# Values' products between the halves of the keys in two decode turns; first norm's sums ahead of the parameters; first values behind gate tiles

## What is computed

```python
h = rmsnorm(x, norm_mix)
proj = h @ w_in        # q, k, v, z, xbc, dt, glu, and 3 x 1024 gate columns
...                    # sample: keys and values of 1024 past positions from pages of 128
z = jnp.einsum('bqhd,bkhd->bhqk', qblk, k) * scale + bias
log_1mb = jnp.where(mask, jax.nn.log_sigmoid(-z), 0.0)
after = lax.cumsum(log_1mb, axis=3, reverse=True) - log_1mb
w = jnp.where(mask, jnp.exp(jax.nn.log_sigmoid(z) + after), 0.0)
out = jnp.einsum('bhqk,bkhd->bqhd', w, v)
...
gates = jax.nn.sigmoid(proj[..., OFF_GATE:].reshape(b, L, N_BRANCH, D_MODEL))
merged = jnp.einsum('blnd,nbld->bld', gates, u)
```

## Time and profile before

| | |
|---|---|
| time of three runs | 910.25, 917.35, 919.32 us (median 917.35) |
| the profiled execution | 910.75 us, of which 909.0 us from first to last instruction |
| PE / weight loads on PE / DVE / ACT / POOL busy | 834.7 / 507.6 / 406.0 / 224.2 / 132.2 us |
| DMA | 190.37 MB, mean 209 GB/s |
| chain of work that ended last | PE 60%, POOL 11%, SP's queue 9%, DVE 7%, issue 4%, DMA 3% |

### The profile page before, as it was taken

One profiled execution on the slowest core, in us unless ns is written; L12 is line 12 of the kernel. 1 busy time (PEld: TensorE's weight loads), 2 busy tenths in 40 slices (PEclk: granted clock), 3 DMA queues, 4 the chain that ended last, 5 costly groups with the idle time before them and its releaser, 6 DMA issues.

```text
span 909.0 us, 12228 instructions
## 1 busy us (share of the span) xinstructions
PE 834.7 (92%) x4488; PEld 507.6 (56%) x4488; DVE 406.0 (45%) x974; ACT 224.2 (25%) x448; POOL 132.2 (15%) x253
## 2 busy tenths in 40 slices
PE   4899999999778989999789999799999999999895
PEld 2577666766556655756347767563444444433474
DVE  2307664467376464342213411713455354454553
ACT  2211534323332243333032012420111111100233
POOL 4002069999200000000000020000000000000000
PEclk9999999999989999999799999989999999999998
DMA  9423312323872445888575100098998998999701
GB/s 266 105 93 133 134 42 92 116 94 94 264 223 68 133 146 194 268 265 268 157 287 198 46 1 1 1 409 351 397 422 334 421 421 362 421 370 424 295 0 61
DMA packets 80047, 190.37 MB, mean 209 GB/s; under 512 B 9033, under 2 KB 33929, under 8 KB 67687
## 3 DMA queue, kind: packets, MB, share of 16 engines
q1 hardware_dynamic: 78034, 184.50, 55.0%
q0 software_dynamic: 1600, 4.34, 1.7%
q10 hardware_dynamic: 349, 0.70, 0.3%
HBM read 184.23 MB, written 5.64 MB: 209 GB/s over the span
## 4 chain that ended last, share of the span: by engine, by line
PE 60%; POOL 11%; SPq 9%; DVE 7%; issue 4%; DMA 3%; ACT 3%; ACTq 0%; DVEq 0%; POOLq 0%
PE bank L2283 13%; POOL ring L646 8%; PE bank L1731 7%; PE bank L2303 7%; PE bank L2080 6%; PE bank L1904 5%; SPq L413 4%; SPq L410 4%; PE bank L2120 4%; PE bank L2194 4%; PE bank L2247 3%; POOL proj L649 2%; DMA ring<-in_state_cf_conv 2%; DMA gate_w<-in_w_in 1%; PE bank L2224 1%
## 5 line engine op out<-in xcount | busy, mean ns | idle before, releaser
L1731 PE MATMUL bank<-scratch,ring 128*128 128x320 f32 x512 | 144.3, 439 | 0.0
L1904 PE MATMUL bank<-scratch,gate_w 128*128 128x320 f32 x384 | 116.4, 460 | 16.0 <-DMA gate_w<-in_w_in 14.7
L2283 PE MATMUL bank<-weights,h_exp 128*64 128x512 f32 (+1 forms) x864 | 126.8, 492 | 1.2 <-DVE rows L1593 1.2
L1731 PEld LDWEIGHTS bank<-scratch,ring 128*128 128x128 f32 x512 | 96.5, 192 | 43.1 <-issue 5.5
L1904 PEld LDWEIGHTS bank<-scratch,gate_w 128*128 128x128 f32 x384 | 76.1, 203 | 50.6 <-DMA gate_w<-in_w_in 16.1
L1600 DVE TENSOR_TENSOR x<-x,bank 128x320 f32<-128x320 f32 x160 | 67.1, 481 | 52.2 <-PE bank L2247 52.2
L2283 PEld LDWEIGHTS bank<-weights,h_exp 128*64 128x64 f32 (+1 forms) x864 | 39.3, 122 | 65.5 <-issue 57.1
L646 POOL TENSOR_SCALAR ring<-scratch,par_w 128x64 f32<-128x64 f32 x120 | 73.1, 637 | 3.0
L2303 PE MATMUL bank<-weights,act_ft 128*64 128x512 f32 (+1 forms) x432 | 61.0, 486 | 0.4 <-DVE act_ft L1617 0.4
L1184 DVE SCALAR_TENSOR_TENSOR proj<-scratch,par_w,proj 128x256 f32<-128x256 f32 x120 | 53.9, 513 | 0.2
L672 POOL MEMSET scratch<- 16x2048 f32 x1 | 1.8, 1794 | 288.8 <-DVE proj L1455 288.8
(11 more groups left out here) (369 smaller groups left out, 1085.9 us busy)
## 6 DMA issues: line engine op xcount, KB each, us to landing
weights<-in_w_expert_gate SPq DMA_DIRECT2D x32, 1024.0 KB, 10.2
weights<-in_w_expert_up SPq DMA_DIRECT2D x32, 1024.0 KB, 12.2
weights<-in_w_expert_down SPq DMA_DIRECT2D x16, 2048.0 KB, 15.3
ring<-in_w_in SPq DMA_DIRECT2D x8, 2048.0 KB, 7.7
ring<-in_cache_k SPq DMA_DIRECT2D x64, 256.0 KB, 3.9
ring<-in_cache_v SPq DMA_DIRECT2D x64, 256.0 KB, 4.1
gate_w<-in_w_in SPq DMA_DIRECT2D x24, 512.0 KB, 6.3
ring<-in_w_branch SPq DMA_DIRECT2D x3, 2048.0 KB, 8.6
```

Source lines behind the costliest of these rows:

```text
L1731: m = MM(bank[b_][:, 0:T], slot(j, DC, GROUP)[:, k, (n % 4) * P:(n % 4 + 1) * P], h[:, k, :], start=k == 0, stop=k == DC - 1)
L1904: m = MM(bank[b_][:, c0:c0 + T], g_w[GW_AT[g]][:, k, :], h[:, k, :], start=k == 0, stop=k == DC - 1)
L2283: m = MM(bank[0][per * p:per * (p + 1), 0:2 * DE // g], h_exp[i % 2][:, k, first_place(n):first_place(n) + per], w_gu[u][:, :, k, columns( ...
```

## The change

At the start, the state_cf_conv load moves from the ACT queue to SP's, ahead of the first two w_in groups, with a semaphore of its own. PE sums the first three pairs of squares before it waits for the other twelve parameters, transposes the first parameters, sums the last pair, and transposes the rest. ACT copies the second block of parameters behind the norm's root.

In the prompt attention, SP issues the weights of gate tiles 3 and 4 ahead of the first values of sequence 0 (before: tile 3 behind them, tile 4 behind those of sequence 1), and tile 5 between the two.

In decode turns 1 and 2 (`WOVEN`), turn_weights, weigh and their gate tile go between score(i, 0) and the second half of the keys; turn_out and the last gate tile go ahead of score(i, 1). ACT's and DVE's copies follow. turn_out writes bank 7 in place of bank 3 in all turns, which takes two waits away and adds one in weigh. SP's loads are re-ordered to suit: gate weights one place earlier, the two sequences' values apart.

```diff
+    WOVEN = range(1, NB // 2 - 1)
...
             sp.dma_start(a_log, a["a_log"][0].unsqueeze(1)).then_inc(s("w_dt_loaded"), 16)
+            sp.dma_start(raw_cf, a["state_cf_conv"][0].rearrange("(a b) t c -> (b t) a c", a=2)).then_inc(s("cf_loaded"), 16)
             w_group(0)
...
             sp.wait_ge(s("slot_stored"), 1)
-            gate_weights(2)
+            for g in range(2, 5):
+                gate_weights(g)
             fetch("v", 0, 0, 2)
-            gate_weights(3)
+            gate_weights(5)
             sp.wait_ge(s("slot_stored"), 2)
             fetch("v", 1, 0, 2)
-            for g in range(4, 11):
+            for g in range(6, 11):
                 gate_weights(g)
...
             gate_weights(12)
-            for i in range(1, NB // 2 - 1):
-                g = 9 + 4 * i
+            gate_weights(13)
+            for i in WOVEN:
+                g = 10 + 4 * i
                 gate_weights(g)
+                gate_weights(g + 1)
                 keys(i + 1, 0)
                 keys(i + 1, 1)
-                gate_weights(g + 1)
+                values(i, 0)
                 gate_weights(g + 2)
-                values(i)
+                values(i, 1)
                 gate_weights(g + 3)
...
-            for g in range(21, 24):
+            for g in range(22, 24):
                 gate_weights(g)
...
+                if i in WOVEN:
+                    biased(i, 0)
+                    if i != 1:
+                        gate_copy(gs[1])
+                    weights_copy(i - 1)
+                    gate_copy(gs[2])
+                    o_copy(i - 1)
+                    for k in range(4, 8):
+                        k_copy(i, k)
+                    gate_copy(gs[3])
+                    biased(i, 1)
+                    exp_abs(i)
+                    log_1p(i)
+                    continue
...
+                if i in WOVEN:
+                    weights_copy(i - 1)
                 for k in range(4, 8):
                     k_copy(i, k)
-                if i:
+                if i in WOVEN:
+                    o_copy(i - 1)
+                elif i:
                     weights_copy(i - 1)
...
-            pe.wait_ge(s("par_loaded"), 13 * 16)
+            pe.wait_ge(s("const"), 2)
+
+            def pair_sum(c):
+                pe.wait_ge(s("norm_paired"), c // 2 + 1)
+                return MM(bank[7][:, 0:T], ones[:, :], h[:, c, :], start=c == 0, stop=c == DC - 2)
+
+            for c in range(0, DC - 2, 2):
+                pair_sum(c)
+            pe.wait_ge(s("par_loaded"), 12 * 16)
             for c in range(DC):
                 m = TR(bank[4][:, 33 * c:33 * (c + 1)], raw_d[:, c * P:(c + 1) * P], ident[0:33, 0:33])
             m.then_inc(s("par_turned"), 1)
+            pair_sum(DC - 2).then_inc(s("norm_summed"), 1)
...
             pe.wait_ge(s("x_ready"), DC)
+            pe.wait_ge(s("cf_loaded"), 16)
...
                 score(i, 0)
+                if i in WOVEN:
+                    if i != 1:
+                        gate_tile(gs[1])
+                    turn_weights(i - 1)
+                    gate_tile(gs[2])
+                    weigh(i - 1)
+                    turn_keys(i, 1)
+                    turn_out(i - 1)
+                    gate_tile(gs[3])
+                    score(i, 1)
+                    continue
                 turn_keys(i, 1)
```

More of the change, by code:

```diff
@@ L419, in keys, with values @@
                 fetch("k", u, i, 0)
-            def values(i):
+            def values(i, u):
                 sp.wait_ge(s("o_done"), i)
-                for u in range(2):
-                    fetch("v", u, i, 2)
+                fetch("v", u, i, 2)
             def ring_load(L, dst, src):
@@ L744, in _ @@
                 F(h[:, c, :], x[:, c, :], ACT.Square).then_inc(s("norm_squared"), 1)
-            act.wait_ge(s("par_turned"), 2)
+            act.wait_ge(s("par_turned"), 1)
             copy(par_d[:, :, :], bank[4][:, 0:DC * 33].rearrange("p (c n) -> p c n", c=DC)).then_inc(s("par_ready"), 1)
-            copy(par_w[:, :, :], bank[5][:, 0:WC * (4 + KC)].rearrange("p (c n) -> p c n", c=WC)).then_inc(s("par_ready"), 1)
             act.wait_ge(s("const"), 1)
             norm_root(0, D)
+            act.wait_ge(s("par_turned"), 2)
+            copy(par_w[:, :, :], bank[5][:, 0:WC * (4 + KC)].rearrange("p (c n) -> p c n", c=WC)).then_inc(s("par_ready"), 1)
             act.wait_ge(s("par_turned"), 3)
@@ L962, in _ @@
                 k_copy(i, 7)
-                if i != 1:
-                    gate_copy(gs[1])
+                gate_copy(gs[1])
                 if i == 0:
@@ L1433, in _ @@
                 later_sums(i)
-                if i:
+                if i and i not in WOVEN:
                     o_copy(i - 1)
@@ L1700, in _ @@
             m.then_inc(s("par_turned"), 1)
-            pe.wait_ge(s("const"), 2)
-            for c in range(0, DC, 2):
-                pe.wait_ge(s("norm_paired"), c // 2 + 1)
-                m = MM(bank[7][:, 0:T], ones[:, :], h[:, c, :], start=c == 0, stop=c == DC - 2)
-            m.then_inc(s("norm_summed"), 1)
             pe.wait_ge(s("x_ready"), DC)
+            pe.wait_ge(s("cf_loaded"), 16)
             for c in range(WC):
@@ L1981, in score @@
                     pe.wait_ge(s("att_ready"), H)
-                if hf and i >= 2:
-                    pe.wait_ge(s("o_copied"), 8 * (i - 1))
                 rows_of = [slice(4 * NT * c, 4 * NT * (c + 1)) for c in range(WC)]
@@ L1988, in score @@
                 if hf:
-                    pe.wait_ge(s("proj_evac"), 33 + GATES_OF[i][1 if i else 2])
+                    pe.wait_ge(s("proj_evac"), 33 + GATES_OF[i][3 if i in WOVEN else 1 if i else 2])
                     for u in range(2):
@@ L2005, in weigh @@
                 pe.wait_ge(s("ln_scaled"), 1)
+                if i:
+                    pe.wait_ge(s("o_copied"), 8 * i)
                 pe.wait_ge(s("turned_copied"), 3 * i + 2)
@@ L2022, in turn_out @@
                 pe.wait_ge(s("turned_copied"), 3 * i + 3)
-                pe.wait_ge(s("z_biased"), 3 * min(i + 2, NB // 2))
-                if i:
-                    pe.wait_ge(s("o_copied"), 8 * i)
                 for c in range(WC):
-                    m = TR(bank[3][:, c * P:(c + 1) * P], o_rows[:, c * P:(c + 1) * P], ident[:, :])
+                    m = TR(bank[7][:, c * P:(c + 1) * P], o_rows[:, c * P:(c + 1) * P], ident[:, :])
                 m.then_inc(s("o_turned"), 1)
@@ L2043, in _ @@
                     norm_sum(2, cf_sq, WC)
-                if i != 1:
-                    gate_tile(gs[1])
+                gate_tile(gs[1])
                 if i == 0:
```

3 lines of the change are left out of this document (1 added, 2 removed).

## The result

The changed kernel takes 926.69 us (median of 4 runs, 924.1 to 928.8), the kernel before, timed in the same rounds, 916.13, a ratio of 1.0128 (interval 1.0096 to 1.0159). That is 11 to 12 us slower, a difference beyond the noise but under 2%. The prediction's time was 927. The profiled execution is the quickest of the four, 924.1 us with a span of 922.4; the sum had given 923.8 for it.

What follows compares the result with a forecast made beforehand. PE was taken as the bound, with time won or lost only where it stands still. Terms -5.2 - 6.3 + 23.6 + 6.4 - 11.3 + 5.8 = +13.0 us gave 927 on the mean, range 915 to 938.

Steps and rivals of the forecast that it cites:

- The keys' wait: Turns 2 and 3: PE idles 11.8 us each for the late key refill, in two pieces; 23.6 us more.
- The floor: Turns 2 and 3: DVE's vector chain before page copies alone would make PE wait 8.1 us each.
- Rival (a): Turns 2 and 3: DVE's chain is the bound, not the refill; +5.6 us, 920; chance 0.13.
- The clock: Behind the new waits of turns 2 and 3: PE runs slow, 3.2 us each, 6.4 us more.
- The removed waits: Turns 1 to 3: waits of 0.99, 0.45, 0.51 and gate 21's 6.21 with 3.16 slow clock go; 11.3 us less.
- gate 22: Gate tile 22: its weights come late, a wait of 3.8 us and some 2 of slow clock; 5.8 us more.
- Gate 3: Prompt attention, gate tile 3: loses its 3.87 us wait and 2.47 of slow clock; 6.3 us less.
- The start: First norm: three sums fill PE's wait for parameters, so w_in's products start earlier; 5.2 us less.
- this case: Start: the eight products behind the sums run at the slow pace, 3.6 us come back; 1.6 us less.
- (b): Turns 2 and 3: the clock stays up through the new waits; 8.4 us less, +4.6, 919; chance 0.13.
- (c): Start and gate tile 3: neither gives any gain; +24.5 us, 939; chance 0.10.
- (d): Turns 2 and 3: the interleaving costs nothing and the gains remain; -17 us, 897; chance 0.04.

Runs made afterwards that it cites:

- The first two experiments: Changed kernel with turns 1 and 2 in the old order: 893.75 us; kernel before with only the interleaved turn order, SP's queue as before: 948.26 us.
- the third: Changed kernel with key pages of turns 2 and 3 fetched from fixed places, without loads of page numbers (a measurement only): 919.81 us, ratio 1.0039.
- the fourth experiment: Changed kernel with products on constant and old data ahead of each key wait of PE in turns 2 and 3: 919.14 us, ratio 1.0047.
- the fifth and sixth experiments: Kernel before with the new start alone: 908.74 us, ratio 0.9936; kernel before with the new order of gate weights 2 to 5 alone: 906.77 us, ratio 0.9898.
- the last experiment: Changed kernel with old turn order, gate 22's weights right behind gate 21's, and constant products keeping PE busy at the start: 891.32 us, ratio 0.974.

## Why the prediction was right, and where its steps were not

**The keys' wait** was the step that carried the sum, and it held: two pieces in turns 2 and 3 (4.86 and 5.19, 4.73 and 6.42 us, for 4.3 and 7.5), released by in_cache_k, 21.2 us for the 23.6 worked out. In turn 2 the first register load of the refill goes out at 345.3 us and the last page has landed at 367.0, 21.7 us for the 22.3 predicted; in turn 3 it is 23.2. The rest of the difference is in the transposes between the two pieces: they already ran at the lower clock (3.25 and 3.65 us for 1.9) while the refill went on, so that part of the idle time turned into slow work. The first two experiments together show that the interleaving alone makes these waits, the third that the refill, with SP's loads of page numbers in it, is their longer condition.

**The floor** behind them, 8.1 us of DVE's chain, was right to a tenth (8.15 and 8.14), though no row of before showed it at those places. Rival (a) had put the total 7.4 us lower if the refill were not the bound; with the loads taken out it came 7 to 8 us lower, though by another sum: 4.9 us of waits and 4.5 of pace, less 1.3 for a slower gate 22. The Trainium skill, "DMA: Bandwidth & Descriptors", section "Issuing engines are not separate DMA queues", calls the sequencer's time to start a DMA usually small relative to the DMA. For a single page that is not far off here: its number and its issue cost SP 1.07 us, and it lands 3.8 us after the issue (median). But the landings overlap and SP's time adds up over 16 pages: taking out the loads alone brought the refill from 21.7 to 14.9 us.

**The clock**, 6.4 us predicted, measured 5.1 by the fourth experiment's rows. The step was mis-sized: it took gate 21's 3.2 us for the waits of a turn, where 2.2 and 2.9 were added behind the second wait. What the transposes behind the first one lost, 1.3 and 1.7 us, was lost inside the refill's time and cost nothing more.

**The removed waits and gate 22** came out as worked out: turn 1 without its 0.99, gate 21 without wait and slow pace, gate 22 late in its place (a wait of 4.51 and 1.6 us of slow pace, for 3.8 and 2). The 17.1 us of fetches ahead of gate 22's weights, which the prediction used and no row shows, are 17.7 in the trace after, from the end of gate 21's issue (439.70) to gate 22's (457.44).

**Gate 3** gave 6.5 us for 6.3, and DVE did not take the wait's place. The 2.25 us of the stretch with gate 2 are not the edit's by any row. SP issues gate 2's weights at the same place in both kernels, as soon as out_k_sample has been stored from its ring slot. That store, before and after, in the chain of work that ended last:

```profile
231.37 4.01 DMA out_k_sample<-ring
...
228.99 3.98 DMA out_k_sample<-ring
```

It began 198.2 us behind the first product of w_in before (231.37 less 33.16), and 197.15 after. Over all nine executions it is 197.1 to 198.8, with the old order of gate weights 3 to 5 (198.2, 197.15, 197.16) as with the new one. So some 1.1 us belong to the one execution of before. The weights land no faster than they did, 4.06 us after their issue for 3.7. Another 1.5 us are the tile's pace, 6.09 for 4.57 us: with the old order it was slow in all three executions, with the new one in two of six. Alone the edit measured 9.3 us; its interval holds 6.3 as well as 6.5 + 2.25, so a gain at gate 2 is not shown.

**The start** is the step that failed against the execution on which the sum was made: -1.3 for -5.2. The working named this case and gave it 1.6: the slow pace that the sums no longer use up is then borne by the dt products. It came so, and a little worse than that bound: of the 3.9 us that are missing, 1.2 lie ahead of the last sum's end (20.49 for 19.3) and 2.7 in the dt products. Yet the term was right for the time: the edit alone measured 5.9 us less over many executions. The two readings go together because the profiled execution of before had left the slow pace early. Its products of w_in start at 33.16; in two other executions with the old start they start at 36.88 and 37.79 (35.9 on the mean). With the new start, and nothing in it to keep PE busy, they start at 31.84, 27.35, 30.72, 29.31 and 30.84 (30.0 on the mean). The step took a pace that differs from execution to execution for one of the kernel's own. That the total was met on the profiled execution is therefore partly luck: 3.9 us were lost there, 2.25 found at gate 2, and 1.7 saved in turn 2, where waits and clock had been put too high.

Of the rivals, (a) fell with in_cache_k as what ended the waits, (b) with the 0.50 in the table by stage, (c) with gate 3 and the fifth and sixth experiments, though its sign at the start, products of w_in not 5 us earlier, did appear in the profiled execution; (d) fell with the first two. The ground given against (b) was weaker than it was put: the clock had not shown its lower pace after every wait of over 3 us, since behind a wait of 3.38 us the dt products took 4.47 us, the same as 16 instructions of this width in an undisturbed gate tile.

## What to carry to other kernels

When work is moved ahead of the last reader of a ring slot, count the refill from that reader to its next use, with the queue's own instructions in it, and put beside it whatever else the moved work used to cover; the longer of the two is the new wait, the shorter its floor. What stands behind the late refill on the same queue becomes late as well. A short stretch at the start of a kernel, or behind a wait, should be costed from more than one execution, since the pace of the same products can differ by a factor of two.

## What the runs showed of the hardware that was not expected

- The start's slow pace lasts for a different time in each execution of the same instructions. The sums and dt products go at about 0.53 or at 0.27 us an instruction (six of the sums take 3.57 us in the changed kernel, 1.88 in the last experiment); with the new start the dt products took 7.22, 4.47, 6.93, 6.16 and 6.99 us in five executions. The profile's column of the granted clock reads 1.00 in these stretches all the same (24.70 to 27.00 us of the changed kernel, within its 7.22), so there the pace is to be read from the durations. They are two to one, as the levels 1.2 and 2.4 GHz are; that it is the clock at the start too is inferred from this ratio and shown by no row.
- Much the same wait does or does not bring the clock down. Ahead of gate tile 2 PE waited 1.81, 2.27, 1.84 and 2.15 us and the tile then took 4.57; it waited 1.86, 2.12, 2.48 and 2.02 us in four other executions and the tile took 6.26 or 6.27. What decides is not shown. A slow tile behind a wait of about 2 us can thus be costed only as a chance, and by itself it makes 1.7 us of difference between two executions.
- A page's number costs SP about 0.55 us and its transfer another 0.52 us of issue, so that the 16 pages of a refill hold the queue for about 17 us however quick the transfers are. Without the numbers the 16 issues went out in 8.48 us, and a transfer then took a little longer to land (4.7 and 4.5 us in the median of turns 2 and 3, where it had been 3.8 and 3.9).
